# Gathering an expert's tokens by features instead of by rows, in a mixture-of-experts kernel

## The reference

```python
def moe_ffn(h, w_router, b_router, w_mlp1, b_mlp1, w_mlp2, b_mlp2):
    logits = (xf @ w_router + b_router)            # 256 x 32
    top_val, top_idx = lax.top_k(logits, TOP_K)    # 4 of 32
    gates = jax.nn.softmax(top_val, axis=-1)
    ...                                            # tokens sorted by expert, in blocks
    def expert_block(args):
        xb, e = args
        hid = xb @ w_mlp1[e] + b_mlp1[e]           # 1024 x 2048
        glu = jnp.minimum(hid[..., ::2], SWIGLU_LIMIT)
        lin = jnp.clip(hid[..., 1::2], -SWIGLU_LIMIT, SWIGLU_LIMIT)
        act = glu * jax.nn.sigmoid(SWIGLU_ALPHA * glu) * (lin + 1.0)
        return act @ w_mlp2[e] + b_mlp2[e]         # 1024 x 1024
    ...                                            # times the gate, summed per token
```

## Time and profile before

| | us |
|---|---|
| median of 3 runs | 1709.08 (1704.43 to 1709.18) |
| profiled execution | 1696.87 |
| its span | 1695.0 |
| PE busy, matmuls | 1610.0 (95%) |
| PE busy, weight loads | 895.2 (53%) |
| DVE busy | 589.3 (35%) |
| ACT busy | 358.6 (21%) |
| DMA, whole span | 545.49 MB, mean 322 GB/s |

### The profile page before, as it was taken

One profiled execution on the slowest core, in us unless ns is written; L12 is line 12 of the kernel. 1 busy time (PEld: TensorE's weight loads), 2 busy tenths in 40 slices (PEclk: granted clock), 3 DMA queues, 4 the chain that ended last, 5 costly groups with the idle time before them and its releaser, 6 DMA issues. The chain is left out here.

```text
span 1695.0 us, 20905 instructions
## 1 busy us (share of the span) xinstructions
PE 1610.0 (95%) x7480; PEld 895.2 (53%) x7480; DVE 589.3 (35%) x1363; ACT 358.6 (21%) x678; POOL 0.2 (0%) x4
## 2 busy tenths in 40 slices
PE   7999989999999988789999988999999999999997
PEld 4888878888888866633333322333333333333332
DVE  3647753689810553321211211111112211212112
ACT  3125563433210243210111101111111110101111
POOL 0000000000000000000000000000000000000000
PEclk9999999999999998979999998999999999999999
DMA  9936675457963420348999999999999999999995
GB/s 396 399 132 253 248 273 187 158 208 306 402 264 128 149 100 1 112 196 361 421 420 420 420 421 420 420 407 421 420 420 420 420 421 400 421 419 420 420 421 230
DMA packets 77222, 545.49 MB, mean 322 GB/s; under 512 B 8945, under 2 KB 9457, under 8 KB 11537
## 3 DMA queue, kind: packets, MB, share of 16 engines
q1 hardware_dynamic: 76048, 542.31, 79.3%
q10 hardware_dynamic: 1024, 1.18, 0.2%
HBM read 542.41 MB, written 1.05 MB: 321 GB/s over the span
## 5 line engine op out<-in xcount | busy, mean ns | idle before, releaser
L1019 PE MATMUL bank<-ring,scr 128*64 128x512 f32 x2048 | 455.4, 600 | 8.5 <-DMA ring<-in_w_mlp 8.5
L516 PE MATMUL bank<-hT,ring 128*128 128x256 f32 x1600 | 351.8, 381 | 0.0
L516 PEld LDWEIGHTS bank<-hT,ring 128*128 128x128 f32 x1600 | 304.8, 191 | 44.8 <-issue 3.7
L1019 PEld LDWEIGHTS bank<-ring,scr 128*64 128x64 f32 x2048 | 145.0, 139 | 302.2 <-issue 272.1
L1052 PE MATMUL bank<-ring,hT 128*64 128x512 f32 x1024 | 233.4, 597 | 1.7 <-DMA ring<-in_w_mlp 1.7
L2329 DVE TENSOR_SCALAR scr<-bank 128x256 f32<-128x256 f32 x64 | 27.0, 422 | 386.2 <-PE bank L1019 386.2
L1052 PEld LDWEIGHTS bank<-ring,hT 128*64 128x64 f32 x1024 | 68.5, 136 | 140.0 <-issue 132.7
L2399 DVE COPY hT<-bank 64x512 f32<-64x512 f32 x32 | 22.2, 695 | 314.5 <-PE bank L1052 284.9
L1542 ACT ACTIVATE scr<-scr 128x256 f32<-128x256 f32 x64 | 26.7, 417 | 494.1 <-DVE scr L2329 494.1
L1667 DVE SCALAR_TENSOR_TENSOR ring<-ring,cb 128x1024 f32<-128x1024 f32 x80 | 94.5, 1219 | 0.0
L728 PE MATMUL bank<-scr,ring 128*128 128x256 f32 x384 | 83.5, 379 | 1.6 <-ACT scr L1381 1.6
(11 more groups left out here) (402 smaller groups left out, 1419.5 us busy)
## 6 DMA issues: line engine op xcount, KB each, us to landing
ring<-in_w_mlp SPq DMA_DIRECT2D x384, 1024.0 KB, 21.6
ring<-in_w_in SPq DMA_DIRECT2D x28, 1024.0 KB, 14.7
ring<-in_up SPq DMA_DIRECT2D x24, 1024.0 KB, 7.1
ring<-in_w_ada SPq DMA_DIRECT2D x24, 1024.0 KB, 6.9
ring<-in_ada_w SPq DMA_DIRECT2D x16, 1024.0 KB, 4.9
ring<-in_down SPq DMA_DIRECT2D x12, 1024.0 KB, 16.7
ring<-in_ada SPq DMA_DIRECT2D x8, 1024.0 KB, 18.7
ring<-in_w2in SPq DMA_DIRECT2D x6, 1024.0 KB, 13.9
```

The costliest lines, as they stand in the source:

```text
L516: ins = mm(b[:, 256 * j:256 * j + 256], v[:, k * 256 + j * 128:k * 256 + j * 128 + 128], rhs[:, k, :], start=(k == 0), stop=(k == 7))
L1019: ins = mm(HID[0][n][64 * hf:64 * hf + 64, :], K.xe[0][x % 2][:, xo:xo + 64], v[:, o0:o0 + 512], start=False, stop=(k == 7), skip_group_ch ...
```

## The change

The gather's operands change places. `gather_columns` lets a 128x128 block of the token rows (128 tokens by 128 features) stand and the 64 columns of the selection move; the result is 128 features by 64 tokens, one chunk of what up wants. Eight chunks by two halves of the tokens are 16 matmuls, which fill bank 3. ScalarE copies it to `xe` at once. `turn_rows`, `xg`, their copy and four semaphores go; up reads chunk k at column 64 k, where before it was at 128 (k % 4) + 64 (k // 4). The second block is changed alike.

```diff
-        self.xg = carve(512)
-    def gather_rows(c):
-        for tt in range(2):
-            for hf in range(2):
-                ins = mm(B[3][64 * hf:64 * hf + 64, :], K.sel[c][:, tt, :], K.h4[:, tt, hf * 512:(hf + 1) * 512],
+    def gather_columns(c):
+        for k in range(8):
+            for tt in range(2):
+                ins = mm(B[3][:, 64 * k:64 * k + 64], K.h4[:, tt, 128 * k:128 * k + 128], K.sel[c][:, tt, :],
                          start=(tt == 0), stop=(tt == 1), skip_group_check=True)
-    def turn_rows():
-        for q in range(4):
-            ins = e.transpose(B[3][:, 128 * q:128 * q + 128], K.xg[:, 128 * q:128 * q + 128], ident)
...
-        gather_rows(0).then_inc(S.m_gath, 1)
-    def gather_turn(x):
-        e.wait_ge(S.m_xg, x + 1)
-        turn_rows().then_inc(S.m_xet, 1)
+        gather_columns(0).then_inc(S.m_gath, 1)
... (TensorE, second_block; up and second_up)
-            gather_rows(1).then_inc(S.n_gath, 1)
-            e.wait_ge(S.n_xg, x + 1)
-            turn_rows().then_inc(S.n_xet, 1)
+            gather_columns(1).then_inc(S.n_gath, 1)
-            xo = 128 * (k % 4) + 64 * (k // 4)
+            xo = 64 * k
... (ScalarE, gather and second_block)
         e.wait_ge(S.m_gath, x + 1)
-        if x:
-            e.wait_ge(S.m_xet, x)
-            e.wait_ge(S.n_xet, x)
-        act(K.xg, B[3][:, :], ACT.Copy).then_inc(S.m_xg, 1)
-    def gather_turn(x):
-        e.wait_ge(S.m_xet, x + 1)
         if x >= 2:
             e.wait_ge(S.m_piece, K.up_at(x - 2) + 8)
         act(K.xe[0][x % 2], B[3][:, :], ACT.Copy).then_inc(S.m_xe, 1)
...
-            act(K.xg, B[3][:, :], ACT.Copy).then_inc(S.n_xg, 1)
-            e.wait_ge(S.n_xet, x + 1)
```

More of the change, by code:

```diff
@@ L121 @@
 ROUND = """
-m_piece m_vec m_sel m_gath m_xg m_selt m_selT m_xet m_xe m_up0 m_glu m_hid m_sig m_actd
+m_piece m_vec m_sel m_gath m_selt m_selT m_xe m_up0 m_glu m_hid m_sig m_actd
 m_at m_aT m_ypa m_ypv m_pair m_left m_rank m_perm m_order
-n_up n_down n_vec n_sel n_gath n_xg n_selt n_selT n_xet n_xe n_glu n_hid n_sig n_actd n_at n_aT n_y n_out
+n_up n_down n_vec n_sel n_gath n_selt n_selT n_xe n_glu n_hid n_sig n_actd n_at n_aT n_y n_out
 """
@@ L952, in turn_gates @@
             ins = e.transpose(B[3][:, 128 * tt:128 * tt + 128], K.selg[c][:, tt, :], ident)
-        return ins
-    def turn_rows():
-        for q in range(4):
-            ins = e.transpose(B[3][:, 128 * q:128 * q + 128], K.xg[:, 128 * q:128 * q + 128], ident)
         return ins
@@ L994, in second_block @@
             e.sem_inc(S.n_gath, 1)
-            e.sem_inc(S.n_xet, 1)
             e.sem_inc(S.n_selt, 1)
@@ L1079, in turns @@
             turn_hidden(0).then_inc(S.m_at, 1)
-        if x + 1 < NE:
-            gather_turn(x + 1)
     def add_pair(p):
@@ L1103, in tensor_program @@
            skip_group_check=True).then_inc(S.m_perm, 1)
-        gather_turn(0)
         gates(0)
@@ L1531, in second_block @@
                 e.wait_ge(S.n_xe, x)
-            e.sem_inc(S.n_xg, 1)
             e.sem_inc(S.n_xe, 1)
```

## The result

| | before | after |
|---|---|---|
| median of the runs, us | 1706.76 (4 runs) | 1750.76 (1748.13 to 1753.48, 4 runs) |
| ratio, 95% interval | | 1.0277 (1.0237 to 1.0318) |
| profiled execution, its span | 1696.87, 1695.0 | 1753.27, 1751.4 |

The change makes the kernel 2.8% slower, 44 us. The prediction had the sign, the resource and most of the mechanism, but 1729 us and a range that ended at 1747.

What follows compares the result with a forecast made beforehand. The new loop over the experts was taken to be bound by PE: +43.2 us of work less 14.6 of waits is +28.6, less 8.7 for slower DMA is +19.9; 1709.1 + 19.9 = 1729 us, range 1713 to 1747.

Steps and rivals of the forecast that it cites:

- What bounds the kernel now: Loop over the experts: the bound changes hands between PE and DMA; only PE's 14.6 us of waits can hide added work.
- The gather: Each expert's gather: loads of 128 standing columns set its pace, 3.65 us where the old one took 1.76.
- the sum: PE work added in the loop: 42.0 for 30 regular experts, 0, 0.2 and 1.0 elsewhere, together +43.2 us.
- Loads and streams add: Rival, 4%: in the gather, load and streaming times add to 5.1 us a gather; about 1774 us in all.
- Expert 0: Loop's start, at half clock: between +1.5 and -4.1 us, taken as 0 since the clock may rise sooner.
- Expert 1: Second expert of the loop: gather +1.9 us, the turn and the wait behind it -1.7, sum +0.2.
- the second gather: Second gather of the two crowded experts: -1.0 to +2.3 us each by the clock, taken as +0.5 each.
- The clock falls: Rival, 5%: the gather lowers the clock to 1.2 GHz in each expert, another 98 us; about 1827 us.
- To the median: Profile to median: the 12.2 us between them is slower DMA; 8.7 of it, the loop's share, would no longer be paid.
- the 28.6: Loop's growth in us: 43.2 of added PE work less 14.6 of waits that hide it.
- Hidden anyway: Rival, 7%: DMA at 420 GB/s hides the added 43 us of PE work in the loop; 1709 to 1714 us.
- Faster: Rival, 3%: the gather's loads hide behind the streaming, 1.7 us a gather; 1702 us in all.

Runs made afterwards that it cites:

- the two doses: Kernel before with each turn of the gathered rows issued twice: ratio 1.0015, median 1709.11 us; kernel before with each gather by rows issued twice: ratio 1.0196, median 1741.86 us.
- a_move32: Changed kernel, but only the first 32 of the 64 places move in the gather: 1806.93 us, ratio 1.0602.
- a_stand64: Changed kernel, but only 64 of each chunk's 128 features stand in the gather: median 1703.65 us, ratio 0.9982.
- a_attn_fill: Changed kernel with 22 extra matmuls of ones in the attention that add nothing to the result: median 1741.89 us.

## Why the prediction was wrong

**"What bounds the kernel now"** held. PE's 14.6 us of waits were all used: none is left in the profile after, the last expert gave back 5.9 us as forecast, and the two doses show the same account by stretches.

**"The gather"** held in kind: the loads of the standing columns set it, by a_move32 and a_stand64. Its size too: 3.65 us was forecast, and 3.72 is measured ahead of down, 3.62 ahead of a pair. A regular expert grew by 1.42 us with a pair (28.20 to 29.62) and 1.71 without one (24.42 to 26.13), mean 1.57 for +1.40. The missing 0.17 is mostly at the neighbours, which the sum left as they were: up takes 13.83 us for 13.74, and the turn that stays 0.59 for 0.49 now that down follows it, so that without the other turn (0.53) only 0.43 us is saved, not 0.49. 30 x 0.17 = 5 us of the 15 missing. The rival "Loads and streams add", 5.1 us a gather, is refuted by 3.7. The sentence of the Trainium skill that stood beside it ("TensorE: Matmul & The Clock Gate", section "The mechanism") so doesn't hold for this form; the same section also lets a load go ahead into a background weight buffer, which would fit, but no run here tells it apart.

**"Expert 0", "Expert 1", "the second gather"** and the sum's silence on the gathers behind crowded experts are the step that failed in the loop: +1.6 for 0, +2.2 for +0.2, +1.7 and +0.8 for +0.5 each, and 2.2 and 3.1 us where nothing was put: 10 us over the sum, in the one profiled execution of each kernel. I had the price at half clock (6.9 us) from the earlier trace rows and took the middle, on the argument that PE without gaps lets the clock rise sooner. The runs show the reverse. Behind the start of the new gather the clock stayed low for 13.0 to 13.4 us in all five traces, behind that of the gather by rows for 2.5 to 3.2 us in seven of eight. The trace I had read from is the eighth, so for expert 0 the half-clock price of +1.5 was simply the right one. Expert 1's +2.2 is the least sure: up(0) to up(1) takes 27.8 us in the profile after, because the clock fell at 774.3 ahead of the matmuls of L1110 (5.8 us), and 25.1 in a_attn_fill. The earlier trace rows held the hint, since the same form ran at half clock there; the rival "The clock falls" read it as staying at 1.00.

**"To the median"** failed outright. I put 12.2 us down to slower DMA and took 8.7 off the answer. They are the clock's ahead of the loop, which falls in some executions of either kernel and not in others, and have no part in the loop. Of the 24 us that the forecast of +19.9 lacks, this choice is 8.7, the clock in the loop 10 and the regular expert 5. Without it the forecast is 1738; with the true regular expert (5 us) and the clock's 10 us the 28.6 become the measured 44.

**The rivals.** "Hidden anyway" would have needed 40 us of waits. "Faster" needed a gather below 2.25 us. "The clock falls" was wrong for the steady experts of this kernel; with 32 moving columns (a_move32) it came true.

## What to carry to other kernels

Count the columns that are loaded, not the products: a gather of 64 tokens by a standing selection loads 8 x 64 columns, by standing tokens 32 x 128, and with 64 moving columns each its streams did not hide those loads here. When a queue of DMA looks full, sum the waits of the engine beside it; here that sum, stretch by stretch, was all that could be hidden. And price new TensorE work at half clock wherever the clock is low ahead of it or the engine has idled, as at the slow gathers here, before explaining a gap between runs by a resource that no row shows.

## What the runs showed of the hardware

TensorE at work all the time doesn't by itself hold its clock. Records of 128 standing and 64 moving columns, 0.116 us apart at full clock, left it at 1.2 GHz from 743.8 to 750.9 and from 1102.0 to 1108.4 and did not lower it from 2.4 GHz in 28 steady experts; with 32 moving columns at the same pace it fell behind the gather (0.63 and 0.52 at 838 to 842). The attention, with many such records, can stay at 0.50 from 638 to 665 us with PE busy throughout (27.00 us of 27.00 in the profile after); in other runs of the same code it doesn't fall there, and why it falls in one and not in another stays open. With 22 small matmuls more all 11 runs are in the lower group, by their times and mean clocks: about 6 us of added work made the kernel 0.5% faster.
